# Routed experts of an encoder layer: gathers issued one block further ahead, and expert weights loaded in one contiguous run per partition

## What is computed

```python
# xt: (T, 1024); idx, w: the 6 experts of each token and their weights
for block of 128 token slots, all of one expert e:
    h = xt[tok] @ w_exp_in[e]            # 1024 x 512
    g, up = split(h)                     # 256 each
    yb = (silu(g) * up) @ w_exp_out[e]   # 256 x 1024
    acc[tok] += yb * gate[:, None]
```

## Time and profile before

| | |
|---|---|
| median of 3 runs | 2742.68 us |
| the profiled execution, its own time | 2749.92 us |
| its span | 2748.1 us |
| mean granted TensorE clock | 0.968 of full speed |
| TensorE matmul busy | 2529.6 us (92%) |
| VectorE, ScalarE, GpSimd busy | 1521.4, 1316.6, 921.2 us |
| DMA | 462.83 MB, mean 168 GB/s |
| chain that ended last: TensorE, DMA, VectorE | 50%, 7%, 5% of the span |

### The profile page before, as it was taken

The page is one execution under the profiler, slowest core; times in us unless marked ns, Lnnn a source line. Parts: engine busy times, 40 slices in busy tenths (PEclk is TensorE's granted clock), DMA queues, the critical chain, the costliest instruction groups (busy, mean ns, idle before and its releaser), DMA issues.

```text
span 2748.1 us, 40274 instructions
## 1 busy us (share of the span) xinstructions
PE 2529.6 (92%) x13039; PEld 1117.0 (41%) x13040; DVE 1521.4 (55%) x2493; ACT 1316.6 (48%) x1618; POOL 921.2 (34%) x1002
## 2 busy tenths in 40 slices
PE   7999999989999999899889989899899999999980
PEld 2345444544554455455433333233333333333320
DVE  4567446779998588787743433333333333332438
ACT  2354254367776311111136556456566566565645
POOL 3001100100000123233445555456455555554533
PEclk9999999999999999999899999999999999999995
DMA  9530110041111412221268799897787788989849
GB/s 355 195 129 27 47 31 16 8 185 36 36 36 59 151 54 62 92 78 58 74 217 256 212 289 287 244 301 208 239 257 213 224 265 253 280 261 289 256 92 367
DMA packets 185917, 462.83 MB, mean 168 GB/s; under 512 B 21612, under 2 KB 46382, under 8 KB 184142
## 3 DMA queue, kind: packets, MB, share of 16 engines
q1 hardware_dynamic: 140990, 329.19, 34.6%
q0 software_dynamic: 44832, 132.39, 19.5%
HBM read 367.01 MB, written 99.22 MB: 170 GB/s over the span
## 4 chain that ended last, share of the span: by engine, by line
PE 50%; DMA 7%; DVE 5%; issue 2%; POOL 1%; SPq 1%; ACT 0%; DVEq 0%; ACTq 0%; POOLq 0%
PE mx_pH L1319 24%; PE mx_pU L1340 11%; DMA ring<-in_w_exp_in 4%; PE mx_pA L1956 3%; PE mx_pL L1956 3%; PE mx_pH L1981 2%; PE mx_pU L2018 2%; PE mx_pB L1298 1%; PE mx_pB L1989 1%; DMA s_acc<-mx_wso,ex_sidx 1%; DVE ring L1437 1%; DVE ring L1432 1%; DMA qT<-in_w_exp_out 1%; PE mx_pU L1966 1%; PE mx_pA L1993 1%
## 5 line engine op out<-in xcount | busy, mean ns | idle before, releaser
L1319 PE MATMUL mx_pH<-ring,mx_wsi 128*64 x1776 | 811.8, 600 | 42.9 <-DVE mx_h L1232 42.2
L1116 POOL DMA_INDIRECT kT<-s_u,ex_gidx x444 | 452.6, 1019 | 136.9 <-issue 135.0
L1319 PEld LDWEIGHTS mx_pH<-ring,mx_wsi 128*64 128x64 f32 x1776 | 242.0, 139 | 497.0 <-issue 496.8
L1320 PE MATMUL mx_pH<-v,mx_wsi 128*64 128x512 f32 x888 | 412.6, 609 | 0.0
L1340 PE MATMUL mx_pU<-qT,mx_hT 128*64 x896 | 402.8, 592 | 2.3 <-ACT mx_hT L1196 2.3
L1341 PE MATMUL mx_pU<-mx_mrow,mx_hT 128*64 128x512 f32 x896 | 402.8, 592 | 0.0
L1320 PE MATMUL mx_pH<-mx_ln,mx_wsi 128*64 128x512 f32 x888 | 399.2, 592 | 0.0
L1228 DVE STREAM_TRANSPOSE mx_wsi<-kT 128x1024 f32<-128x1024 f32 x112 | 139.2, 1243 | 363.4 <-DMA kT<-s_u,ex_gidx 363.2
L1180 ACT ACTIVATE mx_mrow<-qT 128x2048 f32 x111 | 212.0, 1910 | 149.6 <-PE mx_pU L1341 134.4
L1176 ACT ACTIVATE v<-ring 128x1024 f32 x222 | 222.3, 1048 | 116.7 <-SPq L1082 65.0
L1139 POOL DMA_INDIRECT s_acc<-mx_wso,ex_sidx x112 | 182.9, 1633 | 187.7 <-DVE mx_wso L1255 125.8
(11 more groups left out here) (332 smaller groups left out, 4066.2 us busy)
## 6 DMA issues: line engine op xcount, KB each, us to landing
ring<-in_w_exp_in SPq DMA_DIRECT2D x64, 2048.0 KB
qT<-in_w_exp_out SPq DMA_DIRECT2D x64, 1024.0 KB
fr_wq<-in_w_ada SPq DMA_DIRECT2D x32, 512.0 KB, 5.8
s_acc<-s_acc SPq DMA_DIRECT2D x17, 512.0 KB, 4.1
fr_wf<-in_w_in SPq DMA_DIRECT2D x16, 512.0 KB, 5.8
s_u<-v SPq DMA_DIRECT2D x16, 512.0 KB, 2.6
ring<-s_acc SPq DMA_DIRECT2D x16, 512.0 KB, 14.4
y<-ring SPq DMA_DIRECT2D x16, 512.0 KB, 12.3
```

The lines of the kernel that those rows point to most:

```text
L1116: nc.gpsimd.indirect_dma_start(xg[:, u, g, :], None, u2_q, bass.IndirectOffsetOnAxis(ap=gidx[:, u, g:g + 1].bitcast(U32), axis=0)).then_in ...
L1319: nc.tensor.matmul(pH[low, :], xT[:, u, k, low], wi[:, bass.ds(slot, 1), k, :].rearrange("p a f -> p (a f)"), start=(k == 0), stop=(k == K ...
L1320: m = nc.tensor.matmul(pH[high, :], xT[:, u, k, high], own_in(k, k + 1), start=(k == 0), stop=(k == KD - 1))
```

## The change

Weights: the host lays out w_exp_in as (64, 128, 4096) and w_exp_out as (64, 128, 2048), so that what a partition needs lies in one run, and the loads say so on both sides. Gathers: blocks 1 to 4 ahead of the loop; in `add(b)` the index copy and the gathers of block b + 5 stand behind the scatter and go to the buffer 1 - u; GpSimd has a trip count of its own, and its tail outside the loop has six blocks, the first of which still gathers.

```diff
         def load_in(r, src):
-            sp.dma_start(wi[:, r, :, :], src).then_inc(w_in[r], 16)
+            sp.dma_start(wi[:, r, :, :].rearrange("p k f -> p (k f)"), src).then_inc(w_in[r], 16)
 
         def load_out(r, src):
-            sp.dma_start(wo[:, r, :, :], src).then_inc(w_out[r], 16)
+            sp.dma_start(wo[:, r, :, :].rearrange("p c d -> p (c d)"), src).then_inc(w_out[r], 16)
...
-                load_in(r, w_exp_in[bass.ds(q * RING + r, 1)].rearrange("a (k p) f -> p (a k) f", p=P))
+                load_in(r, w_exp_in[bass.ds(q * RING + r, 1)].rearrange("a p f -> p (a f)"))
                 out_place((r - 1) % RING, q + 1 if r else q)
-                load_out(r, w_exp_out[bass.ds(q * RING + r, 1)].rearrange("a (c p) d -> p (a c) d", p=P))
+                load_out(r, w_exp_out[bass.ds(q * RING + r, 1)].rearrange("a p f -> p (a f)"))
...
-        for b in range(2, 4):
-            places(b, b - 2)
-            gather(b, b - 2)
+        for b in range(2, 5):
+            places(b, b % 2)
+            gather(b, b % 2)
...
-        n = pairs(pool)
+        n = pool.value_load(count_d[:, CUMS + 1:CUMS + 2], min_val=MINB - 5, max_val=MAXB - 5) // 2
 
         def add(b, u, more, last=False):
             nc.gpsimd.tensor_copy(sidx[:, u:u + 1], tok[:, bass.ds(b, 1)]).then_inc(sidx_ready, 1)
-            if more:
-                places(b + 4, u)
             pool.wait_ge(sidx_ready, b + 1)
             pool.wait_ge(y_ready, b + 2)
             passed(pool, apart)
             nc.gpsimd.indirect_dma_start(acc_d, bass.IndirectOffsetOnAxis(ap=sidx[:, u:u + 1].bitcast(U32), axis=0), y[:, u, :], None,
                                          compute_op=ALU.add).then_inc(scattered, 16)
             if more:
-                gather(b + 4, u)
+                places(b + 5, 1 - u)
+                gather(b + 5, 1 - u)
...
-        for j in range(4):
-            add(n * 2 + j, j % 2, False, j == 3)
+        for j in range(6):
+            add(n * 2 + j, j % 2, j == 0, j == 5)
...
-                step(nc.vector.tensor_scalar(sm[:, 6:7], done[:, N_EXP - 1:N_EXP], -3.0, None, ALU.add))
-                nc.vector.tensor_copy(cumi[:, CUMS:CUMS + 1], sm[:, 6:7]).then_inc(tables_ready, 1)
+                nc.vector.tensor_scalar(sm[:, 6:7], done[:, N_EXP - 1:N_EXP], -3.0, None, ALU.add)
+                step(nc.vector.tensor_scalar(sm[:, 7:8], done[:, N_EXP - 1:N_EXP], -5.0, None, ALU.add))
+                nc.vector.tensor_copy(cumi[:, CUMS:CUMS + 2], sm[:, 6:8]).then_inc(tables_ready, 1)
...
-        "w_exp_in": w["w_exp_in"].reshape(N_EXP, 4, KD, 32, 2 * D_E).transpose(0, 2, 1, 3, 4).reshape(N_EXP, D, 2 * D_E), "w_exp_out": w["w_exp_out"], "w_sh_in": w["w_sh_in"], "w_sh_out": w["w_sh_out"],
+        "w_exp_in": w["w_exp_in"].reshape(N_EXP, 4, KD, 32, 2 * D_E).transpose(0, 1, 3, 2, 4).reshape(N_EXP, P, KD * 2 * D_E),
+        "w_exp_out": w["w_exp_out"].reshape(N_EXP, D_E // P, P, D).transpose(0, 2, 1, 3).reshape(N_EXP, P, D_E // P * D), "w_sh_in": w["w_sh_in"], "w_sh_out": w["w_sh_out"],
```

More of the change, by code:

```diff
@@ L1089, in sync_part @@
         for r in range(1, RING):
-            load_in(r, w_exp_in[r].rearrange("(k p) f -> p k f", p=P))
+            load_in(r, w_exp_in[r])
             out_place(r - 1, 1)
-            load_out(r, w_exp_out[r].rearrange("(c p) d -> p c d", p=P))
+            load_out(r, w_exp_out[r])
             in_place(r, 1)
@@ L1492, in mixing @@
         tok0 = sb("mx_tok0", [P, 1])
-        cumi = sb("mx_cumi", [P, CUMS + 1], I32)
+        cumi = sb("mx_cumi", [P, CUMS + 2], I32)
         blk = sb("mx_blk", [P, HALVES], I32)
@@ L1599, in _ @@
             sp.wait_ge(pa_mm, NT)
-            sp.dma_start(first_w[:, 0, :, :], exp_weights[0][0].rearrange("(k p) f -> p k f", p=P)).then_inc(w_in_exp[0], 16)
-            sp.dma_start(second_w[:, 0, :, :], exp_weights[1][0].rearrange("(c p) d -> p c d", p=P)).then_inc(w_out_exp[0], 16)
+            sp.dma_start(first_w[:, 0, :, :].rearrange("p k f -> p (k f)"), exp_weights[0][0]).then_inc(w_in_exp[0], 16)
+            sp.dma_start(second_w[:, 0, :, :].rearrange("p c d -> p (c d)"), exp_weights[1][0]).then_inc(w_out_exp[0], 16)
             for r in range(2):
@@ L2098, in program @@
     list_d = scratch("s_list", (N_EXP * T + P, 2), I32)
-    count_d, block_d = scratch("s_count", (1, CUMS + 1), I32), scratch("s_block", (1, HALVES * P), I32)
+    count_d, block_d = scratch("s_count", (1, CUMS + 2), I32), scratch("s_block", (1, HALVES * P), I32)
     shared = ExitStack()
```

## The result

| | before | after |
|---|---|---|
| median of 10 runs each | 2748.14 us (2739.33 to 2750.82) | 2756.2 us (2754.6 to 2763.56) |
| profiled execution, own time | 2749.92 us | 2761.07 us |
| span, mean granted clock | 2748.1 us, 0.968 | 2759.3 us, 0.970 |
| loss of the expert stage | 55.3 us | 63.9 us |

The account below looks back on a forecast made before the run. TensorE's own work, 10.735 us a block, bounds the kernel, with 55.3 us lost mainly to late weights. Gaining 34.5 us less 1.5 at the start nets 33 off the 2742.7 us median: 2709 us, range 2693 to 2734.

Parts of the forecast that it names:

- The account of the loss: Expert stage: 55.3 us lost beyond TensorE's own work, 38.7 in five waits for late weights, 16.1 in slow clock.
- Stalls: Five TensorE waits for weights: three go, that at 2382.24 keeps 1.9 us, that at 1751.74 keeps 11.7.
- Rate: Weight loads in 16 and 8 KB runs move at 422 GB/s: 1.2 us less per expert, 7.5 in all.
- the 34.5 us: Stage gain from earlier weights: four stalls with their clock 36.6 us, plus 1.2, less 3.3.
- Turns: DMA queues alternate by piece; 8 w_in pieces instead of 64 let fewer gather and scatter packets pass: 2.2 us per load.
- the weights starve the scatters: Rival, chance 0.10: scatter packets wait behind 16 KB pieces, GpSimd's round beside weights reaches 13.9 us; 2784 us.
- Gather further ahead: Gathers in the loop issued one block further ahead: 0 us by itself, worth as cover against waits behind 16 KB pieces.
- Start: Block 1's gather waits behind the first three experts' loads: 1.5 us lost, bounds 0 and 4.
- Signs: Trace signs, if right: 128 + 128 packets per expert, hardware queue under 43% of engines, gather waits far below 354 us.
- slower rival's two signs: GpSimd's round beside weights above 12.7 us, and TensorE waiting for VectorE's result.

Follow-up runs that it names:

- e3: Changed kernel with w_in in two 8 KB runs per partition, w_out still 8 KB; 2721.98 us, ratio 0.9905 to the kernel before.
- e2: Kernel before with the new gather order alone, weights in 2 and 4 KB pieces; 2742.65 us, ratio 0.9974 to the kernel before.
- e8: Changed kernel with w_in and w_out in 8 KB pieces and the old gather order; 2747.1 us, ratio 1.001 to the kernel before.
- e9: Changed kernel with the next scatter's index copy issued early, w_in in 8 KB and w_out in 4 KB pieces; 2717.31 us, ratio 0.9903.
- e4: Changed kernel with w_in and w_out in 4 KB pieces; 2724.9 us, ratio 0.9909 to the kernel before.
- e10: Changed kernel with the next scatter's index copy issued early, w_in and w_out in 4 KB pieces; 2725.3 us, ratio 0.9924.
- e6: Changed kernel with the next scatter's index copy issued early and w_in in 8 KB pieces; 2719.6 us, ratio 0.9903.
- e7: Changed kernel with w_in kept in 16 KB pieces and w_out in 4 KB pieces; 2734.9 us, ratio 0.9962 to the kernel before.
- e5: Changed kernel, 16 KB pieces kept, next scatter's index copy issued before the wait for the present one; 2739.42 us, ratio 0.9979.

## Why the prediction was wrong

**The account of the loss** (55.3 us over blocks 1 to 111, TensorE fed late by the weights) held. **Stalls** held in the main: the four are down to 2.5 us and less, the one at 1751.74 is kept at 13.49 us where 11.7 was forecast. **Rate** was sized too large: 43.8% in place of 46.1% of 1200 us is 0.46 us less per expert (0.74 in e3), where 1.2 was forecast. What 8 pieces instead of 64 spare w_in came out right: w_in lands in 9.5 us against 12.2 with 2 KB pieces (e2), 2.7 us earlier. Less than 0.5 of this is rate, so at least 2.2 us are left for the turns, and 2.2 was forecast. A gain like the 34.5 us is there in e3: 32.1 us of stage, 26 us of time. That it lies so near is partly luck, since the sum gave all of it to the weights, and 8 KB pieces without the lead won 7.4 us of stage (e8).

The forecast also stood on a median of three runs, 2742.7 us, 5.5 us under that of ten; that changes nothing of what follows.

**The step that failed is "Turns".** It counted what 8 pieces in place of 64 give to w_in and left the other side of the same alternation, what each scatter packet then waits for, to a rival with 0.10: in the sum the scatters cost nothing. The runs show a round beside weights of 13.04 us in place of 12.24, and a stage 40.7 us longer than with 8 KB pieces. The two queues alternate one for one whatever the sizes. In the kernel before over 2021 to 2023, beside 2 KB pieces, and in the changed kernel over 1617 to 1621 (packets, MB, share):

```profile
q0 software_dynamic: 75, 0.31, 76.7%
q1 hardware_dynamic: 82, 0.17, 27.4%
...
q1 hardware_dynamic: 107, 0.81, 51.5%
q0 software_dynamic: 98, 0.40, 50.9%
```

In the second stretch 91 of the 107 are 8 KB pieces of w_out, 4 are of 16 KB and 12 are small ones. So what most of a scatter's packets waited for was an 8 KB piece of w_out, 324 ns in the median, where it had been a piece of 4 KB (159 ns) or 2 KB (84 ns); the 16 KB pieces (618 ns) count at its start. By the Trainium skill (DMA: Bandwidth & Descriptors, Queues, rings and completion order) an engine takes a whole packet, typically 9 to 17 descriptors, from a queue before it turns; if each piece in these counts is one descriptor, they do not bear the grouping out.

**The rival "the weights starve the scatters"** is what happened. It was to decide from a round of 12.74 us on, with 8.06 without weights. The second number moved as well: in kernels with the new order the fastest rounds without weights are 8.5 to 8.9 us, since the index copy of the gathers, with its wait (0.79 us at 1614.38), now stands behind the scatter. I take 8.5, and the limit becomes (112 x 10.735 - 48 x 8.5) / 64 = 12.4 us. The kernels with the new order, by their measured rounds:

| kernel | round beside weights | loss of the stage |
|---|---|---|
| e9 | 11.42 | 21.1 |
| e4 (4 KB) | 11.78 | 27.2 |
| e10 (4 KB) | 11.80 | 30.8 |
| e6 | 11.93 | 21.7 |
| e2 (2 KB) | 12.30 | 49.0 |
| e3 (8 KB) | 12.33 | 23.2 |
| e7 | 12.46 | 36.2 |
| e5 | 12.68 | 35.5 |
| after (16 KB) | 13.04 | 63.9 |

e2 stands apart: its round is under the limit, VectorE waits for a free y only 4.4 us in all, and it keeps the five long waits of the kernel before, with w_in transfers of 11.4 to 14.5 us on its chain. For the others the loss lies between 21 and 31 us up to 12.33 and doesn't follow the round; the three above 12.4 lie at 35 and more. For the changed kernel (64 x 13.04 + 48 x 8.5) / 112 = 11.1, over 112 blocks some 40 us more than TensorE needs; the loss against e3 is 40.7. So close a match is luck in part: the same sum gives 3 us for e7 and 17 for e5, where 13.0 and 12.3 us over e3 were measured. It gives the order of size and no more. Forecast for the rival were 74 us, from a round of 13.9; with 40 in its place its sum is 2742.7 + 40 - 33 = 2750, and 2756 was measured beside a kernel before of 2748. **Its chance was too low**: the margin was 12.21 against 12.74, 0.5 us, and the bound on the cost 4.2 us. The argument against it, that the transfer is over earlier, doesn't hold for a round whose scatter starts 3 us late and then meets w_out.

**Gather further ahead** at 0 by itself: it was 6.3 us of stage and 7 us of time (e2). As a cover it was right, and larger than was thought: 25 to 28 us. **Start**: 2.65 us where 1.5 was taken and 4 was the bound. **Signs**: packets per expert and the fall of gather waits came as named, the engines' share as 43.8% and not under 43%. Of the slower rival's two signs the round over 12.7 us came. The other, TensorE waiting for VectorE's result (L1254), is in no line of the trace by name; 12.9 us of waits before the second projection stand there without a releaser.

**Open.** TensorE stalls 11 to 14 us near 1750 in every kernel here, with the lead or without. The changed kernel's trace bears out the prediction's reading: SyncE waited 18.7 us for TensorE to free the ring place, and then the load took its 9.99 us (SyncE's wait over 1715 to 1755, then the chain):

```profile
SPq L1075 <- PE mx_pU L1340: 18.7, 1, 18.7
...
1738.30 9.99 DMA ring<-in_w_exp_in
```

That a longer ring or another order of SyncE's loads would remove it is not shown; no run changed either. The gain of e2 is not traced to single stalls, and why 28.4 and not 40.7 us came back in e5 is open too.

## What to carry to other kernels

When two DMA queues share the engines and take turns piece by piece, as here, a bigger piece on one is a longer wait for every packet on the other: cost both sides, and hold the slower side's round against the block time with its margin. Enlarge pieces only as far as their own transfer still gets faster (here 8 KB; 4 KB did as well within the noise), and give what is gathered two blocks of time. A loop one short wait away from being the bound counts as a likely bound.

## What the hardware showed unexpectedly

- w_in took 12.2, 11.0, 9.5 and 9.5 us in pieces of 2, 4, 8 and 16 KB beside gathers. Little of this is rate: in the records a 2 KB piece of w_in took an engine 84 ns in the median (kernel before) and a 16 KB piece 618 (changed kernel), so 64 small pieces are 5.4 us of an engine and 8 large ones 4.9. By the Trainium skill (DMA: Bandwidth & Descriptors, Specifications) line rate is reached from 512 B on; from 8 to 16 KB the trace agrees, while 2 KB pieces move 24 bytes per ns and engine and 16 KB pieces 26.5, some 8% apart.
- Beside weights the first packet of a scatter started 5.2 us after its issue in the median before the change and 5.1 us after it (single ones at 1.6 to 6.1), without weights 2.2 us. These some 3 us are nearly the same with pieces of 2 KB and of 16 KB. So it isn't the turn behind one piece, and no run here shows what it is. It is the larger part of what weights add to a round, 12.2 against 8.1 us before.
- Two changes that each moved the time by +1.3% and -0.3%, or by +0.1% and -0.3% with 8 KB pieces, gave +0.4% and -0.95% together: they don't add, since one is the other's cover.
